# First-pair operands made within the value stage, and the chunk's steps moved to other products, in a hybrid mLSTM and convolution layer

## What is computed

```
s   = einsum('bhtd,bhsd->bhts', qc, kc) * Dm
num = w_int[..., None] * einsum('bhvd,bhtd->bhtv', C, qc) + einsum('bhts,bhsv->bhtv', s, vc)
h   = num / maximum(abs(den), exp(-m_t))[..., None]
C_new = f_end * C + einsum('bhs,bhsv,bhsd->bhvd', w_end, vc, kc)
...
h = h * lax.rsqrt(jnp.mean(h * h, axis=-1, keepdims=True) + EPS)
h = h * head_norm_w * sigmoid(o_pre) * silu(z_m)
```

## Time and profile before

| | |
|---|---|
| median of 3 runs | 2467.45 us (2467.15 to 2469.88) |
| the profiled execution | 2466.87 us, span 2465.1 us, mean granted clock 0.988 |
| TensorE busy | 2361.0 us, 96% of the span |
| VectorE, ScalarE, GpSimd busy | 1501.0, 933.5, 95.1 us |
| stage A, B, C, D | 0 to 225, 234 to 1883, 1894 to 2262, 2266 to 2465 us |
| DMA | 421 MB, mean 171 GB/s |

### The profile page before, as it was taken

One profiled execution on the slowest core, in us unless ns is written; L12 is line 12 of the kernel. 1 busy time (PEld: TensorE's weight loads), 2 busy tenths in 40 slices (PEclk: granted clock), 3 DMA queues, 4 the chain that ended last, 5 costly groups with the idle time before them and its releaser, 6 DMA issues. The chain is left out here.

```text
span 2465.1 us, 41811 instructions
## 1 busy us (share of the span) xinstructions
PE 2361.0 (96%) x14825; PEld 2281.4 (93%) x14825; DVE 1501.0 (61%) x2680; ACT 933.5 (38%) x1701; POOL 95.1 (4%) x82
## 2 busy tenths in 40 slices
PE   7998999999999999999989999999998999999998
PEld 7997999899999999999989999999998999998886
DVE  4334778799876876777557787777654533333333
ACT  4333444344454444444445444444453210011211
POOL 0003000000110000000011000000000000000000
PEclk9998999999999999999999999999998999999999
DMA  6443655455766664565756665565575733344442
GB/s 207 133 131 118 182 195 177 140 181 179 228 224 208 210 202 142 175 182 167 244 161 197 203 221 167 162 191 164 172 211 164 242 118 98 98 131 145 140 141 87
DMA packets 425376, 421.41 MB, mean 171 GB/s; under 512 B 31546, under 2 KB 365498, under 8 KB 425270
## 3 DMA queue, kind: packets, MB, share of 16 engines
q1 hardware_dynamic: 425270, 420.01, 54.5%
HBM read 293.13 MB, written 126.85 MB: 170 GB/s over the span
## 5 line engine op out<-in xcount | busy, mean ns | idle before, releaser
L1485 PE MATMUL b_g<-x_hi,w_hi 128*128 128x344 f32 (+1 forms) x3024 | 989.2, 327 | 28.7 <-DVEq L1107 9.1
L1485 PE MATMUL b_g<-x_lo,w_hi 128*128 128x344 f32 (+1 forms) x3024 | 969.4, 321 | 0.0
L1485 PE MATMUL b_g<-x_hi,w_lo 128*128 128x344 f32 (+1 forms) x3024 | 967.2, 320 | 0.0
L1485 PEld LDWEIGHTS b_g<-x_hi,w_hi 128*128 128x128 f32 x3024 | 571.5, 189 | 38.6 <-issue 10.3
L1485 PEld LDWEIGHTS b_g<-x_lo,w_hi 128*128 128x128 f32 x3024 | 571.8, 189 | 1.7
L1485 PEld LDWEIGHTS b_g<-x_hi,w_lo 128*128 128x128 f32 x3024 | 571.8, 189 | 0.0
L990 ACT ACTIVATE w_hi<-w_operands 128x512 fp32r<-128x512 f32 x533 | 333.7, 628 | 390.0 <-PE b_g L1485 381.6
L1121 DVE TENSOR_TENSOR w_lo<-w_operands,w_hi 128x512 fp32r<-128x512 f32 x533 | 373.1, 711 | 1.8 <-ACT w_hi L990 1.0
L1816 PE MATMUL c_g<-act_hi,RH 128*128 128x294 f32 x896 | 268.8, 300 | 10.5 <-DVE act_lo L1766 10.5
L1816 PE MATMUL c_g<-act_hi,RL 128*128 128x294 f32 x896 | 268.7, 300 | 0.0
L1816 PE MATMUL c_g<-act_lo,RH 128*128 128x294 f32 x896 | 268.3, 299 | 0.0
(11 more groups left out here) (258 smaller groups left out, 2598.5 us busy)
## 6 DMA issues: line engine op xcount, KB each, us to landing
w_operands<-w_in SPq DMA_DIRECT2D x288, 256.0 KB, 5.2
w_operands<-w_ops_d SPq DMA_DIRECT2D x36, 768.0 KB, 4.8
stages<-w_ops_d SPq DMA_DIRECT2D x36, 768.0 KB, 4.9
stages<-w_in SPq DMA_DIRECT2D x72, 256.0 KB, 3.1
w_operands<-w_ops_d SPq DMA_DIRECT2D x72, 256.0 KB, 6.3
w_ops_d<-w_operands SPq DMA_DIRECT2D x18, 768.0 KB, 3.3
w_ops_d<-stages SPq DMA_DIRECT2D x18, 768.0 KB, 3.5
w_ops_d<-w_operands SPq DMA_DIRECT2D x36, 256.0 KB, 3.9
```

Of the source, the lines that this page charges most:

```text
L1485: last = nc.tensor.matmul(bank[:, 0:n], w[:, j, k, :], x[:, k, 0:n], start=(j < 4 and k == 0 and m == 0), stop=(k == 3 and m == 2), skip_g ...
```

## The change

Stage A: the loads of the four token quarters are issued between the bodies of tiles 5 and 6. The first pair's weight sums come before GpSimd's last two powers; the splits of the first pair's weights and of the first token operand come before tile 16; all four token sums are made by GpSimd in stage A, and the second token operand is split there too, before the last bank is emptied. The last v rows go to a buffer of their own, and the wait for their store moves from the end of stage A to the load of pair 2. Stage B: `decode_inputs` is issued one body earlier. In the chunk k is turned at 1, the weighted k is made at 2, P at 3, the heads are at 4, 6, 8, 9, the norm's first step is at 10, ScalarE scales the four rows of h at 12, TensorE turns them by transposes at 13, and the products by the gate come behind the body's last step (at 14).

```diff
@@ phase_a, over_tiles
+        prepare()
         body(NT - 1, 0)
@@ phase_a, SyncE
-            over_tiles(sp, body)
-
+            for i in range(2, 6):
+                body(i, i % 2)
             n = PASSES[0][1]
             for par in range(2):
-                sp.wait_ge(x_stored[par], 16 * (NT // 2))
+                sp.wait_ge(x_stored[par], 48)
             for slot, k0, c0, m in ((0, 0, 0, n), (1, 0, n, n - NS), (2, 4, n, n - NS), (4, 4, 0, n)):
                 sp.dma_start(quarter(g, 0, slot)[:, :, 0:m],
                              g.xT_d[k0:k0 + 4, :, c0:c0 + m].rearrange("k p n -> p k n")).then_inc(xs_in, 16)
-
+            with sp.Fori(3, 7) as j:
+                body(2 * j, 0)
+                body(2 * j + 1, 1)
+            for i in range(NT - 3, NT):
+                body(i, i % 2)
...
             store(NT - 1, 0)
-            sp.wait_ge(v_stored[0], seen(NT - 1, 0))
-            sp.wait_ge(v_stored[1], seen(NT - 2, 1))
@@ phase_a, GpSimd
+            pool.wait_ge(lo_used, 1)
+            pool.wait_ge(s_set, 6)
+            nc.gpsimd.tensor_tensor(a, c, d, ALU.subtract).then_inc(s_set, 1)
+            pool.wait_ge(lo_used, 2)
+            pool.wait_ge(s_set, 7)
+            nc.gpsimd.tensor_tensor(d, quarter(g, 0, 4), d, ALU.subtract).then_inc(s_set, 1)
@@ phase_a, ScalarE and VectorE
+            over_tiles(act, body, first_operands)
+            act.wait_ge(s_set, 6)
+            nc.scalar.activation(g.X1H[:, :, 0:PASSES[0][1]], quarter(g, 0, 3), ACT.Copy).then_inc(hi_set, 1)
+            act.wait_ge(lo_used, 3)
             evac(NT - 1, 0)
+            over_tiles(dve, body, first_operands)
+            dve.wait_ge(hi_set, NOP + 2)
+            nc.vector.tensor_tensor(g.X1L[:, :, 0:n], quarter(g, 0, 3), g.X1H[:, :, 0:n].bitcast(F32), ALU.subtract).then_inc(lo_used, 2)
@@ phase_b, SyncE
+                    if pair == 2:
+                        sp.wait_ge(g.v_stored[0], 16 * (NT // 2 + 1))
-                if extra == "dec_first":
+                if extra == "dec_inputs":
                     decode_inputs()
@@ phase_b, start of the stage
-            x_difference(0)
-            x_late(0)
-            for j in range(1, NOP):
+            for j in range(2, NOP):
                 x_high(0, j)
-            for j in range(1, NOP):
+            for j in range(2, NOP):
                 x_low(0, j)
-                if j < 3:
-                    sums(1, 0, 1, j - 1)
+                if j in (3, 4):
+                    sums(1, 0, 1, j - 3)
@@ phase_b, chunk on ScalarE
+    HEADS = (4, 6, 8, 9)
+                elif at == 12:
+                    act.wait_ge(rs_set, c + 1)
+                    for h in range(NH):
+                        last = nc.scalar.activation(HB[:, h, :], HB[:, h, :], ACT.Copy, scale=ss[:, 2, h:h + 1])
+                    last.then_inc(hn_set, 1)
@@ phase_b, chunk on VectorE
                 if at == 0:
-                    dve.wait_ge(ht_done, 1 + c)
-                elif at == 1:
+                elif at == 2:
 ...
-                elif at == 2:
+                elif at == 3:
 ...
-                elif at == 11:
+                elif at == 10:
 ...
-                elif at == 12:
-                    dve.wait_ge(rs_set, c + 1)
-                    for h in range(NH):
-                        last = nc.vector.tensor_scalar(Dm[:, h, :], g.ident[:, :], ss[:, 2, h:h + 1], None, ALU.mult)
-                    last.then_inc(hn_set, 1)
-                elif at == 13:
+                elif at == 14:
                     dve.wait_ge(ht_done, 1 + c + 1)
@@ phase_b, body on VectorE, behind both pairs
+                if extra == "chunk":
+                    chunk(chunk_of(p, s, i), 14)
@@ phase_b, chunk on TensorE
                     last.then_inc(s_done, 1)
+                elif at == 1:
                     pe.wait_ge(hg_set, 1 + c)
...
                 elif at == 13:
                     pe.wait_ge(hn_set, c + 1)
                     for k in range(KB):
-                        last = nc.tensor.matmul(PT[k // 4][:, k % 4, :], HB[:, k // 2, (k % 2) * P:(k % 2 + 1) * P], Dm[:, k // 2, :],
-                                                start=True, stop=True)
+                        last = nc.tensor.transpose(PT[k // 4][:, k % 4, :], HB[:, k // 2, (k % 2) * P:(k % 2 + 1) * P], g.ident[:, :])
```

More of the change, by code:

```diff
@@ L129, in build @@
         g.X0L = sbuf(nc, early, "x_lo0", [P, 4, TQ], F32R)
+        g.X1H = sbuf(nc, early, "x_hi1", [P, 4, TQ], F32R)
+        g.X1L = sbuf(nc, early, "x_lo1", [P, 4, TQ], F32R)
+        g.v_stored = [early.enter_context(nc.semaphore(f"a_v_stored{j}")) for j in range(2)]
         with early:
@@ L207, in phase_a, with rows_of_v, over_tiles @@
     w_v = g.w_in[0].rearrange("(k p) n -> k p n", p=P)
-    def over_tiles(eng, body):
+    last_rows = g.W7[0][0][:, 4:6].rearrange("p j k n -> p (j k n)")
+    def rows_of_v(i, par):
+        return last_rows if isinstance(i, int) and i == NT - 1 else v_out[par]
+    def over_tiles(eng, body, prepare=lambda: None):
         body(2, 0)
@@ L231, in store @@
                 sp.wait_ge(v_dve, i + 1)
-                sp.dma_start(g.v_rows[at(i), :], v_out[par][:rows(i), 0:D]).then_inc(v_stored[par], 16)
+                sp.dma_start(g.v_rows[at(i), :], rows_of_v(i, par)[:rows(i), 0:D]).then_inc(v_stored[par], 16)
             load_x(0, 0)
@@ L269, in _ @@
                              g.xT_d[k0:k0 + 4, :, c0:c0 + m].rearrange("k p n -> p k n")).then_inc(xs_in, 16)
+            with sp.Fori(3, 7) as j:
[3 more added lines that the diff above has]
+                body(i, i % 2)
+            for par in range(2):
+                sp.wait_ge(x_stored[par], 16 * (NT // 2))
+            sp.wait_ge(v_stored[0], seen(NT - 3, 0))
+            sp.wait_ge(v_stored[1], seen(NT - 2, 1))
             store(NT - 1, 0)
-            sp.wait_ge(v_stored[0], seen(NT - 1, 0))
-            sp.wait_ge(v_stored[1], seen(NT - 2, 1))
         @block.gpsimd
@@ L290, in _ @@
             rstd(1, 1)
-            over_tiles(pool, rstd)
+            rstd(2, 0)
+            with pool.Fori(0, 6) as j:
+                rstd(2 * j + 3, 1)
+                rstd(2 * j + 4, 0)
             pool.wait_ge(w0_in, 64)
@@ L362, in body, with first_operands @@
                 evac(i - 1, 1 - par)
[L364 to L369, removed]
+            def first_operands():
+                act.wait_ge(s_set, 4)
+                for j in range(NOP):
+                    nc.scalar.activation(g.LH[:, j], g.W7[0][0][:, j], ACT.Copy).then_inc(hi_set, 1)
+                act.wait_ge(xs_in, 64)
+                nc.scalar.activation(g.X0H[:, :, 0:PASSES[0][1]], quarter(g, 0, 0), ACT.Copy).then_inc(hi_set, 1)
+            over_tiles(act, body, first_operands)
+            act.wait_ge(s_set, 6)
+            nc.scalar.activation(g.X1H[:, :, 0:PASSES[0][1]], quarter(g, 0, 3), ACT.Copy).then_inc(hi_set, 1)
+            act.wait_ge(lo_used, 3)
             evac(NT - 1, 0)
@@ L422, in body, with first_operands @@
                 evac(i - 1, 1 - par)
[L424 to L427, removed]
             n = PASSES[0][1]
-            dve.wait_ge(hi_set, NOP + 1)
-            nc.vector.tensor_tensor(g.X0L[:, :, 0:n], quarter(g, 0, 0), g.X0H[:, :, 0:n].bitcast(F32), ALU.subtract)
+            def first_operands():
+                for j in range(NOP):
+                    dve.wait_ge(hi_set, j + 1)
+                    ins = nc.vector.tensor_tensor(g.LL[:, j], g.W7[0][0][:, j], g.LH[:, j].bitcast(F32), ALU.subtract)
+                dve.wait_ge(hi_set, NOP + 1)
+                nc.vector.tensor_tensor(g.X0L[:, :, 0:n], quarter(g, 0, 0), g.X0H[:, :, 0:n].bitcast(F32), ALU.subtract).then_inc(lo_used, 1)
+            over_tiles(dve, body, first_operands)
+            dve.wait_ge(hi_set, NOP + 2)
+            nc.vector.tensor_tensor(g.X1L[:, :, 0:n], quarter(g, 0, 3), g.X1H[:, :, 0:n].bitcast(F32), ALU.subtract).then_inc(lo_used, 2)
+            dve.wait_ge(lo_used, 3)
+            dve.wait_ge(s_set, 4)
             evac(NT - 1, 0)
@@ L485, in phase_b @@
     LH, LL = g.LH, g.LL
-    OH = [g.X0H] + [sbuf(nc, ctx, f"x_hi{j}", [P, 4, TQ], F32R) for j in range(1, NOP)]
-    OL = [g.X0L] + [sbuf(nc, ctx, f"x_lo{j}", [P, 4, TQ], F32R) for j in range(1, NOP)]
+    OH = [g.X0H, g.X1H] + [sbuf(nc, ctx, f"x_hi{j}", [P, 4, TQ], F32R) for j in range(2, NOP)]
+    OL = [g.X0L, g.X1L] + [sbuf(nc, ctx, f"x_lo{j}", [P, 4, TQ], F32R) for j in range(2, NOP)]
     P1 = sbuf(nc, ctx, "part1", [P, TQ])
```

38 lines of the change are left out of this document (20 added, 18 removed).

## The result

The changed kernel takes 2483.3 us (median of 8 runs, 2477.8 to 2492.4), the kernel before on the same chips 2467.3 (2465.8 to 2469.9): a ratio of 1.0068, 95% interval 1.0055 to 1.0082. It is slower by 16 to 17 us, where 14 were predicted. The profiled execution took 2477.8 us with a span of 2476.1, so it is the fastest of the eight, 5.5 us under their median; its rows show a little less than the usual loss. The runs also lie further apart than before, 15 us against 4.

A forecast was written before the change was run, and what follows sets the result against it. TensorE is busy 96% of the span, so only its gaps, its own work and the clock count. Terms -16.8 + 4.5 - 3.5 + 19 + 19 - 7.8 - 7.9 + 7.6 = +14 give 2481.5 us, range 2452 to 2492.

The forecast's parts named there:

- the last head: Head 3 in six gates bodies: it no longer waits for ScalarE's copy of head 2, -3.5 us.
- start of stage B: Start of stage B: no store landing awaited, pair 1's weights sooner, product 5 nearer; -7.8 us (-10.5 to -4).
- turning h, scaling: Chunks: eight transposes replace sixteen matmul records, -16.8 us; ScalarE's four copies replace VectorE's diagonals, +4.5 us.
- head 0, waiting: Chunks: P comes later on VectorE, so TensorE waits longer ahead of head 0; +19 us (-5 to +25).
- clock at head 0: Gaps ahead of head 0: TensorE's clock falls behind the long ones, +19 us (0 to +37).
- chunk part with the last head: All chunk edits together, head 3's shorter wait included: +22 us.
- sample inputs: Sample tokens' inputs loaded one body earlier: the 4.93 us gap and its clock loss go, -7.9 us (-8 to -3).
- tile 7: Value stage: four quarter loads delay x tile 7, TensorE waits and its clock falls; +7.6 us (0 to 8.5).
- place of the operands: SBUF place of the second token operand's tiles, read in stage B: given no price, 0 us.
- The rival that it holds: Clock stays up at head 0's gaps: -5 us in all, 2462.5 us; chance 0.24.
- Two of three of 12 gaps at 2.4 us: Clock falls assumed at head 0's long gaps, the basis of that term's +19 us.
- ScalarE's scaling: Chunks: TensorE waits some 1.2 us for ScalarE's copies, +12 us; chunk 6 gains about -7; together +4.5.

The follow-up runs named there:

- 5: Experiment 1 with h turned by transposes and its rows scaled by four ScalarE copies instead of VectorE's diagonals: 2450.4 us, 0.9915 to 0.9942 of the kernel before.
- experiment 1: Changed kernel with the whole chunk part put back as before, the other edits kept: 2463.5 us, 0.9977 to 0.9994 of the kernel before.
- experiment 2: Changed kernel with TensorE doing eight unused matmuls ahead of its wait for P in each chunk: 2463.1 us, 0.9975 to 0.9993 of the kernel before.
- 3: Changed kernel with P alone moved from step 3 to step 2, right behind the weighted q: 2436.6 us, 0.9862 to 0.9891 of the kernel before.
- 7: Changed kernel with P at step 2 and the sample tokens' input loads put back one body later: 2445.2 us, 0.9891 to 0.9921 of the kernel before.
- experiment 4: Changed kernel with the four token quarter loads spread over value-stage bodies 6 to 9: 2473.8 us, 1.0022 to 1.0051 of the kernel before.
- 6: Changed kernel with P at step 2 and the gate products back at product 13: 2427.4 us, 0.9822 to 0.9849 of the kernel before.
- experiment 9: Changed kernel with P early, gate products at 13, quarters spread, and operand tiles 2 to 6 again six tiles apart: 2414.7 us, 0.9773 to 0.9800 of the kernel before.

## Why the prediction was right

The total was right by 2 us (2481.5 for 2483.3), by the mechanism that was forecast: head 0 behind a late P, and the clock behind the gap. Every priced part lies within some 2 us of what was measured, which is also about the error of these differences. One cost of 5 us was missing, and the priced parts came out together some 2 us cheaper than they were put, so that the total hides part of it.

The measured parts, with the last head at its -3.5 (rows show 1.9 us of it, the waits that are gone), add up to -14 + 17 + 20 - 3.5 - 8 + 8.5 - 8.5 + 5 = 16.5, the slowdown of the medians. That the sum fits is no test of its own: the start of stage B is put at what experiment 1 leaves for it, and the 5 us for the operands are read from their pace.

| step | predicted | measured, from |
|---|---|---|
| turning h, scaling | -16.8 + 4.5 | -14 (5 less 1) |
| head 0, waiting | +19 | +17.1 (waits 40.8 less 23.7) |
| clock at head 0 | +19 | +20 (2, and what is left of 3's 47 behind 26.5 of waiting) |
| chunk part with the last head | +22 | +20 (changed less 1) |
| sample inputs | -7.9 | -7.4 to -8.6 (7) |
| tile 7 | +7.6 | +7.6 to +9.5 (4), 9.2 in the trace |
| start of stage B | -7.8 | -8.5 (left over, below), -6.0 in the trace |
| place of the operands | 0 | +5 (from the pace, below) |

**Head 0.** The order on VectorE was the mechanism, and the working holds step by step. With the scores' start (1558.08) as 0, Dm starts at 2.42 (predicted 2.44), ScalarE's L1047 at 5.61 (5.65), L1196 at 6.18 (6.15), P at 11.16 (11.3) and head 0 at 12.14 (12.2). The gap is 3.15 where 3.2 stood. Experiments 3 and 6 show its two halves, the three instructions ahead of P and the gate products ahead of Dm.

**The clock** was the open term (0 to +37) and the one that turned the sign. The rival that it holds is refuted by experiment 2: without the falls the changed kernel takes 2463, as that rival said (2462.5). "Two of three of 12 gaps at 2.4 us" came out well in sum, and that it did is luck in part: no row stood behind the share that was taken, and the kernel's own runs lie 15 us apart. By the distances of head 0's starts the clock fell at seven of them in the profiled execution, at 1.3 to 2.7 us each, some 13 us; this is the fastest run, and the median is 5.5 us more. The price behind it has a small slip: a stretch from 458 to 459 at 0.69 behind the lower level puts the rise at 458.6 and not 458.3, and the loss at 3.3 us and not 3.1.

**ScalarE's scaling.** 0.9 us of wait in all 16 chunks, 13.7 in all, where 1.2 was estimated; there it was a bit too dear, and chunk 6 gave its 5.7 back as said. The prediction's own parts, +12 and -7, make +5 and not the +4.5 that it sums with.

**Start of stage B.** Product 5 stands 8.6 us nearer to the end of the value stage, for 10.3 predicted: pair 1's weights landed at 245.84, 8.7 us into the stage for 7.4. Behind it the clock fell as said, and by the first product of the second pair (262.26, before 259.07) 6.0 us of the 8.6 are left in this execution. With the other terms at their measured size experiment 1 leaves for this one -3 + 8 - 8.5 - 5 = -8.5.

**Place of the operands** is the step that failed, with the price of nothing. The prediction took moving the second operand's two tiles to an earlier allocation for free. It slows the products of passes 0 and 1 by 0.7% (894 to 888) over 72 pairs of some 13.2 us, +6.4, and pass 2 is faster by about 1.5. That is an estimate from the pace; setting the distance right again brought 2.5 us by the ratios (experiment 9), with an error larger than that. The missing cost was within the error of the total.

## What to carry to other kernels

Before moving instructions between engines or steps, write out the in-order queue of the engine that feeds the wait: here the one product that head 0 was moved by (1.9 us) paid for the three instructions that then stood ahead of its operand (1.9 us), and nothing paid for the two gate products (1.2 us). Price a wait on TensorE twice, its length and the clock behind it, and if a gap of some 3 us can't be removed, fill it with harmless matmuls: that gave 20 us here. Look at whether a loss comes from the idea or from its place in the order: the same edit with P one step earlier is 30 us faster than the kernel before instead of 16 slower.

## What the runs showed of the hardware

- Like gaps do not cost alike. Of bodies with the same gap of 3.1 us some keep the clock at 1.00 and some fall to 1.2 GHz, and which ones differs from execution to execution: the clock fell at seven heads in the profile of the changed kernel and at eight in that of experiment 4, whose chunks are the same. The one gap of 2.36 us (chunk 7) was followed by a fall in the first and not in the second; gaps of 2.33 us (chunk 0, both) and 2.25 held. A kernel with such gaps spreads by 15 us, without them by 5. Behind the gaps of up to 1.7 us at head 0 of the kernel before and of experiments 1, 2, 3 and 5 there was no fall.
- The pace of matmuls without any gap depends on where the two moving operands that TensorE reads in turn lie in SBUF: 887 to 894 matmuls in 140 us, 1.900 us for a product with the two side by side and 1.880 with them six tiles apart. 0.7% is small, but it lasts for as long as the products do.
- An x load issued behind four larger loads waits for its turn: it is issued at 85.28 us, 1.1 us behind the fourth, and lands at 95.2, 1.3 us behind the fourth, 9.9 us after its issue where 4.3 is usual. The Trainium skill (DMA: Bandwidth & Descriptors, "Queues, rings and completion order") has the rule, descriptors in ring order, and the trace agrees.
